# Four expert keys computed ahead in the tail of the routing, and the last table part stored in two halves

## Chip, core and metric

The kernel runs on one core of one Trainium2 chip. The time is the device time of one launch in microseconds (us), and lower is better. The weight matrices, the token rows and the output lie in HBM. A core has five engines with their own instruction streams: PE (TensorE), DVE (VectorE), ACT (ScalarE), POOL (GpSimd) and SP (SyncE, which here only issues DMAs). They meet through semaphores.

## What is computed

One decoder layer on 512 tokens of width 2048: a token mixer (attention beside a recurrence), and then a channel mixer with retrieved experts (PEER). The change touches only the channel mixer:

```python
q = (xt @ w_q).reshape(T, PEER_HEADS, 2, PEER_DHALF)
s = jnp.einsum('thcd,hcnd->thcn', q, sub_keys)
# top 16 of 128 in each half, 256 sums, top 16 of those
eidx = jnp.take_along_axis(cidx, top_pos, axis=-1)
gates = jax.nn.softmax(top_s, axis=-1)
a = jnp.einsum('td,ted->te', xs, u[es])
hact = jax.nn.gelu(a) * gs
return jnp.einsum('te,ted->td', hact, v[es])
```

There are 8 heads, 128 x 128 = 16384 experts, and each token picks 8 x 16 of them.

## The kernel before

For 384 of the 512 tokens the kernel doesn't gather experts. It computes all 16384 densely, and multiplies the activations by a table of gates that is zero where a token did not pick an expert. The experts are walked by their first index, a "key" of 128 experts. The last 128 tokens are done sparsely: POOL gathers the rows of u and of v that they picked (512 KB each time, called a task), and DVE multiplies and sums them.

Every f32 operand of a matmul is split into a high part (ACT, a cast to fp32r) and a low part (POOL or DVE, a subtraction). Each product is three matmuls: high by high, and the two mixed ones.

Three stages follow each other around the change. Each is a block with a stream of its own for each engine, and no engine starts a block before all have finished the one before.

**`route` (L1385 to L1622).** Eight heads. `w_q` is streamed in 512 KB steps, four a head: `Stream` has four raw slots and two slots for the parts; SP loads (L284), ACT makes the high part (`split_high`, L305), POOL the low part (`split_low`, L319, 2.4 us each), PE multiplies (L350 to L352) and releases the parts' slot (`used`). PE then forms the scores (L1459), ACT copies them out (L1492), DVE picks the 16 best and their places (L1537 to L1595), POOL weighs the one-hot places with the indices (`weigh`, L1432) and DVE sums them (`keep`, L1553). PE is done with a head about a head before DVE is. After head 7 DVE subtracts the largest score, ACT takes the exponential (L1519), and DVE divides (L1620 to L1622).

**`gate_table` (L1639 to L1738).** The gates are turned (L1669), and for every 16 tokens DVE (L1699, L1704) and ACT (`match`, L1718 and L1722) build one-hot rows, PE multiplies them (L1678), and ACT copies the result into one of two stages (L1734). 24 rounds of 16 tokens are 6 parts of 64 tokens. When a part is complete, SP stores its stage to `gate_table` in HBM: 4 MB, 32 KB in a row from each partition. The first four raw chunks of the next stage are loaded at the start of this block (`load_first_experts`): u keys 0 and 1.

**`experts` (L1752 to L2034).** 32 macros of four keys. PE does the four u steps (activations of a key: 48 matmuls, L1900 to L1902), then four v steps (output columns, 36 matmuls each, L1919 to L1923). For each key ACT takes the gelu (L1960), DVE multiplies by the gates (L2025), ACT and DVE split the result (L1966, L2030). The gates of a key are a DMA from the table (L1852), 768 pieces of 256 bytes. DVE also makes the low part of every u and v chunk (L1984), adds the output banks into `h` (L2014) and does two sparse tasks per step, 16 a macro, in a written order: in each of 8 steps its splits come first, its additions next, its tasks last. Four row buffers hold gathered rows; a gather (L1879) waits until the task four before it is done. Steps 0 to 7 of the order are named in `SPLITS`: v0, u2, u3, v1, u4, v2, v3, u5; u4 and u5 are the first keys of the next macro.

Of the kernel before, what the change touches and what calls it, by code (L numbers as in the profile page):

```python
# [24 lines left out]
ALU = mybir.AluOpType  # L25
# [237 lines left out]
class Stream:  # L263
# [79 lines left out]
    def parts(self, g, c):  # L343

        return self.hi[:, g % 2, c], self.lo[:, g % 2, c]

# [1035 lines left out]
def route(nc, place, kb, stream, xT, picks, cst, plain_stored):  # L1382


    with ExitStack() as ctx:  # L1385
# [27 lines left out]

        def each_head(eng, head, peeled):
# [7 lines left out]
        @block.sync  # L1422
        def _(sp):
            stream.load_rest(sp, PH)

        @block.gpsimd
        def _(pool):
# [16 lines left out]
            each_head(pool, head, 2)  # L1444
            weigh(PH, 0)
            weigh(PH + 1, 1)

        @block.tensor
        def _(pe):
# [30 lines left out]

            each_head(pe, head, 4)
            scores(PH, 1)

        @block.scalar
        def _(act):
# [8 lines left out]
            def head(m, s, first, last=False):  # L1494
# [6 lines left out]
                if not last:  # L1501
                    stream.split_high(act, m + 1, 0)
# [13 lines left out]
            head(PH - 1, 1, False, True)  # L1516
            empty_scores(PH, 1)
            act.wait_ge(shifted, 1)
            act.activation(picks[2][:, :, :], picks[2][:, :, :], ACT.Exp).then_inc(exp_done, 1)  # L1519

# [112 lines left out]
def gate_table(nc, place, stages, stored, hot, picks, picksT, table, cst, at_turned, sparse):  # L1633
# [5 lines left out]
    with ExitStack() as ctx:  # L1639
# [8 lines left out]
        gaps = place("table_gaps", [P, 2, SLOT_TOKENS, NK], F32, 88)  # L1648
# [5 lines left out]
        @block.sync  # L1654
        def _(sp):
            sp.wait_ge(turned, 3)
            sp.wait_ge(picks_kept, 2)
            at_turned(sp)
            with sp.Fori(0, PARTS // 2) as q:
                for s in range(2):  # L1660
                    sp.wait_ge(banks_out, q * (2 * slots_of_part) + (slots_of_part * (s + 1) + SLOTS))
                    sp.dma_start(table[q * 2 + s], stages[s][:]).then_inc(stored[s], 16)
# [48 lines left out]
        def _(act):  # L1711
# [16 lines left out]
            for q in range(PARTS):  # L1728
                if q >= 2:
                    act.wait_ge(stored[q % 2], 16 * (q // 2))  # L1730
                with act.Fori(0, TABLE_TOKENS // run) as i:
                    for s in range(SLOTS):
# [4 lines left out]
                        if s % 2:  # L1737
                            rounds = TABLE_TOKENS // run * q + 1  # L1738
                            match(s, i * run + rounds * run, i * 2 + (2 * rounds + s // 2 + 1))
# [11 lines left out]
RAW_SLOTS, ROW_SLOTS, NOW = 4, 4, 4  # L1751
SPLITS = (("v", 0), ("u", 2), ("u", 3), ("v", 1), ("u", 4), ("v", 2), ("v", 3), ("u", 5))  # L1752


def experts(nc, place, h, xT, raw, loaded, loads, table, table_stored, out, sparse):
# [11 lines left out]
    with ExitStack() as ctx:  # L1767
# [37 lines left out]

        def split_of(m, step):

            kind, which = SPLITS[step]
# [465 lines left out]
```

## Time and profile before

| what | us |
|---|---|
| median of 3 runs | 3561.41 |
| lowest and highest run | 3547.05, 3562.57 |
| the profiled execution | 3550.87 |
| its span, from first to last instruction | 3549.1 |
| routing's last score matmul begins | 1236.6 |
| table block begins | 1276.3 |
| last table store issued | 1418.0 |
| expert block begins | 1419.9 |
| end of the span | 3549.1 |

Times inside the kernel are counted from the first instruction of the profiled execution, which took 3550.87 us by the same clock as the runs. It is 10.5 us below the median of the three runs. A row of the timeline gives a start, a duration, the engine, the line and what was written from what; a wait ahead of it stands in brackets with the engine that ended it.

### The profile page before, as it was taken

What the parts mean: (1) busy time and instruction counts of PE and PEld (TensorE: products, weight loads), DVE (VectorE), ACT (ScalarE), POOL (GpSimd) and SP (SyncE); (2) the same over time, 40 slices, a digit from 0 to 9 for tenths busy, and PEclk for the clock granted to TensorE, in tenths of its full rate; (3) what the DMA queues carried; (4) which work ended last, traced back from release to release, by engine and by line L of the source; (5) the groups of instructions that cost most, each with busy time, mean ns of one, the idle gap of its engine ahead of it and who ended that gap; (6) DMA issues with size and microseconds to landing.
All of it is one profiled execution on the core that took longest, in us unless ns stands there. A gap on an engine that the chain in (4) does not pass through costs nothing.

```text
span 3549.1 us, 51460 instructions
## 1 busy us (share of the span) xinstructions
PE 3359.0 (95%) x16926; PEld 2944.6 (83%) x16926; DVE 2226.8 (63%) x3877; ACT 1116.9 (31%) x1732; POOL 1165.7 (33%) x870
## 2 busy tenths in 40 slices
PE   7999999878989947999999999999999999999999
PEld 5778876667877746898998998998998998999998
DVE  2003412795028898677777777777777777777776
ACT  3122223443232259322233233222332232222322
POOL 2344431264435410322322323323333333323332
PEclk9999999899999979999999999999999999999999
DMA  4223320002332124888887887888888887888876
GB/s 140 73 87 95 95 83 21 25 1 101 95 107 81 56 94 184 316 265 265 268 267 259 274 265 262 270 265 263 271 264 265 269 267 262 271 267 263 269 262 234
DMA packets 276021, 686.85 MB, mean 194 GB/s; under 512 B 120544, under 2 KB 120800, under 8 KB 273504
## 3 DMA queue, kind: packets, MB, share of 16 engines
q1 hardware_dynamic: 202224, 417.51, 36.3%
q0 software_dynamic: 73728, 268.47, 22.5%
q8 instruction: 38, 0.62, 0.1%
q14 instruction: 31, 0.25, 0.0%
HBM read 655.48 MB, written 30.41 MB: 193 GB/s over the span
## 4 chain that ended last, share of the span: by engine, by line
PE 59%; ACT 2%; issue 1%; DMA 1%; ACTq 0%; DVE 0%; DVEq 0%; SPq 0%
PE exp_a L1900 10%; PE exp_a L1902 10%; PE exp_a L1901 10%; PE exp_o L1921 10%; PE exp_o L1923 10%; PE exp_o L1919 10%; ACT table_gaps L1718 1%; ACT table_stage L1734 1%; DMA gate_table<-table_stage 0%; PE table_b L1678 0%; ACTq L1718 0%; DMA exp_raw<-in_v 0%; ACTq L1734 0%; DVE table_hot L1704 0%; PE table_t L1669 0%
## 5 line engine op out<-in xcount | busy, mean ns | idle before, releaser
L1900 PE MATMUL exp_a<-x_high,exp_uh 128*128 128x384 f32 x2048 | 686.4, 335 | 10.6 <-DVE exp_ul L1984 10.6
L1902 PE MATMUL exp_a<-x_high,exp_ul 128*128 128x384 f32 x2048 | 686.0, 335 | 0.0
L1901 PE MATMUL exp_a<-x_low,exp_uh 128*128 128x384 f32 x2048 | 686.0, 335 | 0.0
L1923 PE MATMUL exp_o<-exp_vh,exp_al 128*128 128x512 f32 x1536 | 598.2, 389 | 0.0
L1921 PE MATMUL exp_o<-exp_vl,exp_ah 128*128 128x512 f32 x1536 | 598.1, 389 | 0.0
L1919 PE MATMUL exp_o<-exp_vh,exp_ah 128*128 128x512 f32 x1536 | 597.5, 389 | 0.0
L1879 POOL DMA_INDIRECT exp_rows<-in_v_rows,exp_now x256 | 329.0, 1285 | 707.9 <-DVE h L2005 656.4
L1879 POOL DMA_INDIRECT exp_rows<-in_u_rows,exp_now x256 | 299.5, 1170 | 733.5 <-DVE exp_rows L1998 688.5
L1949 ACT CAST exp_vh<-exp_raw 128x1024 fp32r<-128x1024 f32 x256 | 260.1, 1051 | 516.4 <-PE exp_o L1923 493.1
L1984 DVE TENSOR_TENSOR exp_vl<-exp_raw,exp_vh 128x1024 fp32r<-128x1024 f32 x256 | 304.5, 1220 | 165.7 <-ACT exp_vh L1949 165.7
L1900 PEld LDWEIGHTS exp_a<-x_high,exp_uh 128*128 128x128 f32 x2048 | 385.8, 188 | 12.3 <-DVE exp_ul L1984 7.3
L1901 PEld LDWEIGHTS exp_a<-x_low,exp_uh 128*128 128x128 f32 x2048 | 385.7, 188 | 1.2
L1902 PEld LDWEIGHTS exp_a<-x_high,exp_ul 128*128 128x128 f32 x2048 | 385.7, 188 | 0.0
L1960 ACT ACTIVATE exp_act<-exp_a 128x384 f32<-128x384 f32 x128 | 63.0, 492 | 963.4 <-PE exp_a L1902 963.4
L1923 PEld LDWEIGHTS exp_o<-exp_vh,exp_al 128*128 128x128 f32 x1536 | 288.4, 188 | 59.9
L1921 PEld LDWEIGHTS exp_o<-exp_vl,exp_ah 128*128 128x128 f32 x1536 | 288.4, 188 | 59.2
L1919 PEld LDWEIGHTS exp_o<-exp_vh,exp_ah 128*128 128x128 f32 x1536 | 288.4, 188 | 59.1
L1984 DVE TENSOR_TENSOR exp_ul<-exp_raw,exp_uh 128x1024 fp32r<-128x1024 f32 x256 | 309.7, 1220 | 41.7 <-ACT exp_uh L1949 31.6
L319 POOL TENSOR_TENSOR w_in_lo<-w_in_raw,w_in_hi 128x1024 fp32r<-128x1024 f32 x88 | 212.7, 2418 | 333.3 <-ACT w_in_hi L305 333.3
L2005 DVE SCALAR_TENSOR_TENSOR h<-exp_rows,exp_weights,h 128x1024 f32<-128x1024 f32 x256 | 316.5, 1276 | 0.0
L1998 DVE SCALAR_TENSOR_TENSOR exp_rows<-exp_rows,sparse_x 128x1024 f32<-128x1024 f32 x256 | 302.2, 1216 | 0.0
L2025 DVE TENSOR_TENSOR exp_act<-exp_act,exp_gates 128x384 f32<-128x384 f32 x128 | 71.8, 561 | 360.3 <-ACT exp_act L1960 360.3
(290 smaller groups left out, 5180.6 us busy)
## 6 DMA issues: line engine op xcount, KB each, us to landing
exp_raw<-in_u SPq DMA_DIRECT2D x256, 512.0 KB, 5.2
exp_raw<-in_v SPq DMA_DIRECT2D x256, 512.0 KB, 4.4
w_in_raw<-in_w_in SPq DMA_DIRECT2D x88, 512.0 KB, 3.6
gate_table<-table_stage SPq DMA_DIRECT2D x6, 4096.0 KB, 11.6
exp_gates<-gate_table SPq DMA_DIRECT2D x128, 192.0 KB, 5.3
w_out_raw<-in_w_out SPq DMA_DIRECT2D x32, 512.0 KB, 3.6
w_q_raw<-in_w_q SPq DMA_DIRECT2D x32, 512.0 KB, 3.9
x_rows<-in_x SPq DMA_DIRECT2D x4, 1024.0 KB, 7.9
```

Source lines behind the costliest of these rows:

```text
L319: eng.tensor_tensor(self.lo[:, g % 2], self.raw[:, g % RAW], self.hi[:, g % 2].bitcast(F32), ALU.subtract).then_inc(self.low, 1)
L1879: pool.indirect_dma_start(rows[slot][:, :], None, sparse["u" if kind == "dot" else "v"], bass.IndirectOffsetOnAxis(ap=now[:, turn, place_n ...
L1900: pe.matmul(bank, uh[:, b, c, :], xh[:, 0:DENSE_TB, c, :], start=(c == 0), stop=False)
L1901: pe.matmul(bank, uh[:, b, c, :], xl[:, 0:DENSE_TB, c, :], start=False, stop=False)
L1902: last = pe.matmul(bank, ul[:, b, c, :], xh[:, 0:DENSE_TB, c, :], start=False, stop=(c == DC - 1))
L1919: pe.matmul(bank[:, :], ah[:, key, tokens], vh[:, dc % 2, key, :], start=(key == 0), stop=False)
L1921: pe.matmul(bank[:, :], ah[:, key, tokens], vl[:, dc % 2, key, :], start=False, stop=False)
L1923: last = pe.matmul(bank[:, :], al[:, key, tokens], vh[:, dc % 2, key, :], start=False, stop=(key == KEYS_OF_MACRO - 1))
L1949: act.copy(part(uh if split[0] == "u" else vh, *split, half), raw[:, c % RAW_SLOTS, :])\
L1984: dve.tensor_tensor(part(ul if kind == "u" else vl, kind, which, half), raw[:, slot, :], part(uh if kind == "u" else vh, kind, which, half ...
L1998: done = dve.scalar_tensor_tensor(rows[slot][:, :], rows[slot][:, :], 1.0, sparse["x"][:, half, :], ALU.mult, ALU.mult, accum_out=dots[:, ...
L2005: done = dve.scalar_tensor_tensor(sums, rows[slot][:, :], weights[:, pl(pick(m, kind, t), 1)], sums, ALU.mult, ALU.add)
```

## The change

The first four u keys are computed in `route`, after head 7. They are further steps of the `w_q` stream (a "head" 8 and 9 of four steps each, a step being half a key). SP loads them, ACT makes eight more high parts, POOL eight more low parts between and behind its last two `weigh`, and PE multiplies them into the four `route_q` banks. ACT's gelu writes the four activations to a new buffer `early_act`. The score matmuls of head 7 stand behind the first half key, ACT's exponential behind all the high parts.

`experts` then starts macro 0 with its v steps. Its first four raw chunks are v columns 0 and 1. DVE multiplies the four activations by their gates, then splits them; POOL's gathers wait until that is done. In `gate_table` the last round has no `match` (it had been computed for tokens that don't exist), and the last of the six parts is stored in two halves of 32 tokens. A half is no longer one run per partition: for each of 16384 pairs of indices it takes 32 of 64 tokens, that is 128 bytes.

```diff
 # route: SP, POOL
+            for key in range(EARLY):
+                for half in range(2):
+                    stream.load_row(sp, *early_step(key, half), u[key, :, half * (D // 2):(half + 1) * (D // 2)])
...
             each_head(pool, head, 2)
+            stream.split_low(pool, *early_step(0, 0))
+            stream.split_low(pool, *early_step(0, 1))
             weigh(PH, 0)
+            stream.split_low(pool, *early_step(1, 0))
+            stream.split_low(pool, *early_step(1, 1))
+            stream.split_low(pool, *early_step(2, 0))
             weigh(PH + 1, 1)
+            stream.split_low(pool, *early_step(2, 1))
+            stream.split_low(pool, *early_step(3, 0))
+            stream.split_low(pool, *early_step(3, 1))
 # route: PE
+            def early_key(key):
+                bank = q_bank[key // 2][key % 2][:, 0:TD].rearrange("p (b t) -> p b t", t=P)
+                pe.wait_ge(q_out, 2 * PH + key - 3)
+                for half in range(2):
+                    p, g = early_step(key, half)
+                    stream.await_step(pe, p, g)
+                    for at in range(DC // 2):
...
+                        last = pe.matmul(bank, low, xh, start=False, stop=(c == DC - 1))
+                    stream.release(last)
+                    if key == 0 and half == 0:
+                        scores(PH, 1)
...
-            scores(PH, 1)
+            for key in range(EARLY):
+                early_key(key)
 # route: ACT, after the eight high parts
             act.wait_ge(shifted, 1)
             act.activation(picks[2][:, :, :], picks[2][:, :, :], ACT.Exp).then_inc(exp_done, 1)
+            for key in range(EARLY):
+                open_early(key)
 # gate_table: SP
-                    sp.dma_start(table[q * 2 + s], stages[s][:]).then_inc(stored[s], 16)
+            for q in range(PARTS):
+                pieces = 2 if q == PARTS - 1 else 1
+                count = TABLE_TOKENS // pieces
+                for k in range(pieces):
+                    sp.wait_ge(banks_out, slots_of_part * q + slots_of_part // pieces * (k + 1) + SLOTS)
+                    tokens = slice(k * count, (k + 1) * count)
+                    sp.dma_start(table[q][:, :, tokens], stages[q % 2][:, :, tokens]).then_inc(stored[q % 2], 16)
 # experts: POOL, ACT, DVE
+            pool.wait_ge(a_split, EARLY)
             run(pool, macro)
...
-                act.copy(part(uh, "u", n // 2, n % 2), raw[:, n, :]).then_inc(high, 1)
+                act.copy(part(vh, "v", n // 2, n % 2), raw[:, n, :]).then_inc(high, 1)
+            for key in range(EARLY):
+                act.wait_ge(weighted, key + 1)
+                act.copy(ah[:, key, :], early[:, key, :]).then_inc(a_high, 1)
...
-                low_part("u", n // 2, n % 2, n, n + 1)
+                low_part("v", n // 2, n % 2, n, 2 * EARLY + n + 1)
+            for key in range(EARLY):
+                dve.wait_ge(gates_in[key % 2], 16 * (key // 2 + 1))
+                dve.tensor_tensor(early[:, key, :], early[:, key, :], gates[:, key % 2, :], ALU.mult)\
+                    .then_inc(weighted, 1)
+            for key in range(EARLY):
+                dve.wait_ge(a_high, key + 1)
+                dve.tensor_tensor(al[:, key, :], early[:, key, :], ah[:, key, :].bitcast(F32),
+                                  ALU.subtract).then_inc(a_split, 1)
```

What stands in a row on POOL at the end of the routing, before (`route_hot` is a `weigh`, the branch the end of the block):

```order
217 L318 REGISTER_ALU
218 L319 TENSOR_TENSOR w_q_lo<-w_q_raw,w_q_hi 128x1024
219 L1418 REGISTER_ALU
220 L1418 COMPARE_AND_BRANCH
221 L1432 TENSOR_TENSOR route_hot<-route_hot,route_idx_f 128x1024 x4
222 L1385 UNCONDITIONAL_BRANCH
```

and now:

```order
219 L1439 REGISTER_ALU
220 L1439 COMPARE_AND_BRANCH
221 L319 TENSOR_TENSOR w_q_lo<-w_q_raw,w_q_hi 128x1024 x2
222 L1456 TENSOR_TENSOR route_hot<-route_hot,route_idx_f 128x1024 x2
223 L319 TENSOR_TENSOR w_q_lo<-w_q_raw,w_q_hi 128x1024 x3
224 L1456 TENSOR_TENSOR route_hot<-route_hot,route_idx_f 128x1024 x2
225 L319 TENSOR_TENSOR w_q_lo<-w_q_raw,w_q_hi 128x1024 x3
226 L1402 UNCONDITIONAL_BRANCH
```

Three low parts of the early keys stand behind the last `weigh`, with the matmuls that need them.

On ACT at the same place, before:

```order
411 L1506 COPY route_qT<-route_q 128x512
412 L1508 COPY route_qT<-route_q 128x512
413 L1492 COPY route_scores<-route_s 128x512 x2
414 L1519 ACT_TABLE_LOAD
415 L1519 ACTIVATE picks_80<-picks_80 128x512
416 L1385 UNCONDITIONAL_BRANCH
```

and now:

```order
411 L1556 COPY route_qT<-route_q 128x512
412 L1558 COPY route_qT<-route_q 128x512
413 L305 CAST w_q_hi<-w_q_raw 128x1024
414 L1543 COPY route_scores<-route_s 128x512 x2
415 L305 CAST w_q_hi<-w_q_raw 128x1024 x6
416 L1581 ACT_TABLE_LOAD
417 L1581 ACTIVATE picks_80<-picks_80 128x512
418 L1569 ACT_TABLE_LOAD
419 L1569 ACTIVATE early_act<-route_q 128x384 x4
420 L1402 UNCONDITIONAL_BRANCH
```

Six high parts and a second load of function tables stand around the exponential, and the four gelus behind it.

On DVE at the start of the expert block and in macro 0, now (`exp_dots` are the sparse tasks, `h` the additions of output banks):

```order
726 L2073 TENSOR_TENSOR exp_vl<-exp_raw,exp_vh 128x1024 x4
727 L2143 TENSOR_TENSOR early_act<-early_act,exp_gates 128x384 x4
728 L2147 TENSOR_TENSOR exp_al<-early_act,exp_ah 128x384 x4
729 L2087 SCALAR_TENSOR_TENSOR exp_rows_9797,exp_dots<-exp_rows_9797,sparse_x 128x1024
...
736 L2087 SCALAR_TENSOR_TENSOR exp_rows_9800,exp_dots<-exp_rows_9800,sparse_x 128x1024
737 L2073 TENSOR_TENSOR exp_ul<-exp_raw,exp_uh 128x1024 x2
738 L2087 SCALAR_TENSOR_TENSOR exp_rows_9797,exp_dots<-exp_rows_9797,sparse_x 128x1024
739 L2087 SCALAR_TENSOR_TENSOR exp_rows_9798,exp_dots<-exp_rows_9798,sparse_x 128x1024
740 L2073 TENSOR_TENSOR exp_vl<-exp_raw,exp_vh 128x1024 x2
741 L2103 TENSOR_TENSOR h<-h,exp_o 128x512 x3
```

Between the early keys' split (row 728) and the low parts of v2 (row 740) there are ten tasks and the low parts of u4; before, the splits and the gate products of keys 2 and 3 stood between the same tasks.

## Rows read from the trace of the kernel before

**Rows 1.** The page: the span, and the busy share of the engines.

```profile
span 3549.1 us, 51460 instructions
PE 3359.0 (95%) x16926; PEld 2944.6 (83%) x16926; DVE 2226.8 (63%) x3877; ACT 1116.9 (31%) x1732; POOL 1165.7 (33%) x870
```

**Rows 2.** Busy time by stretch; PEclk is the granted clock, 1.00 is 2.4 GHz.

```profile
core 0: us, PE busy (x) PEld busy (x) DVE busy (x) ACT busy (x) POOL busy (x), PEclk, DMA share, GB/s
1241.00:1272.00 31.00, 0.00 (x0) 0.00 (x0) 26.91 (x117) 0.63 (x1) 9.73 (x4) 0.54 0.00 0
1282.00:1420.00 138.00, 101.48 (x768) 92.29 (x768) 128.14 (x428) 134.87 (x343) 0.09 (x1) 0.97 0.42 175
1445.00:1511.00 66.00, 65.65 (x326) 60.03 (x327) 51.83 (x74) 19.64 (x25) 21.89 (x19) 0.97 0.86 295
```

**Rows 3.** What PE waited for: us in total, times, longest.

```profile
PE table_t L1669 <- PEq L1385: 37.8, 1, 37.8
PE exp_a L1900 <- DVE exp_ul L1984: 10.6, 2, 7.1
```

**Rows 4.** Timeline of the routing's end, engine by engine.

```profile
1236.62 2.05 PE L1459 MATMUL route_s<-sub_keys,route_qT 128*128 128x128 f32 x16
1238.71 0.58 ACT L1492 COPY route_scores<-route_s 128x512 f32<-128x512 f32 x1 [0.31 <-PE route_s L1459]
1239.32 1.28 ACT L1519 ACT_TABLE_LOAD   x1
1269.64 0.63 ACT L1519 ACTIVATE picks<-picks 128x512 f32<-128x512 f32 x1 [29.04 <-DVE picks L1616]
1225.81 2.40 POOL L319 TENSOR_TENSOR w_q_lo<-w_q_raw,w_q_hi 128x1024 fp32r<-128x1024 f32 x1 [0.41 <-ACT w_q_hi L305]
1266.72 5.08 POOL L1432 TENSOR_TENSOR route_hot<-route_hot,route_idx_f 128x1024 f32<-128x1024 f32 x2 [18.66 <-DVE route_hot L1595]
1243.24 1.64 DVE L1537 MAX8 route_val<-route_scores 128x8 f32<-128x128 f32 x8
1276.32 0.29 DVE L1685 SCALAR_TENSOR_TENSOR sparse_experts<-picks,picks 128x128 uint32<-128x128 f32 x1 [0.31 <-PEq L1385]
```

**Rows 5.** Timeline of the table's end.

```profile
1414.90 1.28 ACT L1718 ACTIVATE table_gaps<-c_iota,table_minus 128x128 f32<-128x128 f32 x4
1416.75 1.05 ACT L1734 COPY table_stage<-table_b 128x512 f32 x2
1414.11 1.16 PE L1678 MATMUL table_b<-table_hot 128*128 128x128 f32 x8 [0.74 <-ACT table_hot L1722]
1395.66 22.65 SPq L1662 DMA_DIRECT2D gate_table<-table_stage  x2
1417.97 0.33 SPq L1662 DMA_DIRECT2D gate_table<-table_stage  x1
1431.67 0.82 SPq L2204 DMA_DIRECT2D exp_raw<-in_v  x2
```

**Rows 6.** DMA queues, issues with median us to landing, and shortest landings (gates, gathers).

```profile
q1 hardware_dynamic: 202224, 417.51, 36.3%
q0 software_dynamic: 73728, 268.47, 22.5%
gate_table<-table_stage SPq DMA_DIRECT2D x6, 4096.0 KB, 11.6
c_ln_mix<-in_ln_mix SPq DMA_DIRECT2D x1, 8.0 KB, 2.5
DMA to landing us min/median/max: 3.6/5.3/11.5
DMA to landing us min/median/max: 4.3/5.4/11.7
```

**Rows 7.** Timeline of the experts' start.

```profile
1422.37 0.69 PE L1900 MATMUL exp_a<-x_high,exp_uh 128*128 128x384 f32 x1 [7.11 <-DVE exp_ul L1984]
1427.98 0.35 PE L1902 MATMUL exp_a<-x_high,exp_ul 128*128 128x384 f32 x1
1463.72 0.49 ACT L1960 ACTIVATE exp_act<-exp_a 128x384 f32<-128x384 f32 x1 [5.53 <-PE exp_a L1902]
1496.20 0.33 PE L1900 MATMUL exp_a<-x_high,exp_uh 128*128 128x384 f32 x1
```

**Rows 8.** The page's groups: busy, mean ns of one.

```profile
L1949 ACT CAST exp_vh<-exp_raw 128x1024 fp32r<-128x1024 f32 x256 | 260.1, 1051 | 516.4 <-PE exp_o L1923 493.1
L1984 DVE TENSOR_TENSOR exp_vl<-exp_raw,exp_vh 128x1024 fp32r<-128x1024 f32 x256 | 304.5, 1220 | 165.7 <-ACT exp_vh L1949 165.7
L1998 DVE SCALAR_TENSOR_TENSOR exp_rows<-exp_rows,sparse_x 128x1024 f32<-128x1024 f32 x256 | 302.2, 1216 | 0.0
L2025 DVE TENSOR_TENSOR exp_act<-exp_act,exp_gates 128x384 f32<-128x384 f32 x128 | 71.8, 561 | 360.3 <-ACT exp_act L1960 360.3
```

More of the change, by code:

```diff
@@ L1492, in empty_scores, with head @@
                     act.copy(sc[:, 2 * s + k], s_bank[s][k][:, :, :]).then_inc(s_out, 1)
-            def head(m, s, first, last=False):
+            def head(m, s, first):
                 if not (first and m == 0):
@@ L1500, in head @@
                 stream.split_high(act, m, 3)
-                if not last:
-                    stream.split_high(act, m + 1, 0)
+                stream.split_high(act, m + 1, 0)
                 act.wait_ge(q_done, m + 1)
@@ L1730, in _, with empty @@
                     act.wait_ge(stored[q % 2], 16 * (q // 2))
-                with act.Fori(0, TABLE_TOKENS // run) as i:
+                rounds = TABLE_TOKENS // run
+                def empty(i, with_match):
                     for s in range(SLOTS):
@@ L1736, in _ @@
                             .then_inc(banks_out, 1)
-                        if s % 2:
-                            rounds = TABLE_TOKENS // run * q + 1
-                            match(s, i * run + rounds * run, i * 2 + (2 * rounds + s // 2 + 1))
+                        if s % 2 and with_match:
+                            begun = rounds * q + 1
+                            match(s, i * run + begun * run, i * 2 + (2 * begun + s // 2 + 1))
+                last = q == PARTS - 1
+                with act.Fori(0, rounds - last) as i:
+                    empty(i, True)
+                if last:
+                    empty(rounds - 1, False)
 HALF_D = D // 2
@@ L1751, with experts @@
 RAW_SLOTS, ROW_SLOTS, NOW = 4, 4, 4
+STORES = PARTS // 2, PARTS // 2 + 1
+EARLY_STEPS = range(4)
 SPLITS = (("v", 0), ("u", 2), ("u", 3), ("v", 1), ("u", 4), ("v", 2), ("v", 3), ("u", 5))
[L1755 removed]
+def experts(nc, place, h, xT, raw, loaded, loads, table, table_stored, out, sparse, early):
     xh, xl = xT
@@ L1928, in macro @@
             def macro(m, kind):
-                for key in range(KEYS_OF_MACRO):
-                    u_step(m, key)
+                if not is_first(m):
+                    for key in range(KEYS_OF_MACRO):
+                        u_step(m, key)
                 for dc in range(D // PC):
                     v_step(m, dc)
+            pe.sem_inc(a_done, EARLY)
             run(pe, macro)
@@ L1955, in macro @@
                     done = m * KEYS_OF_MACRO + (key + 1)
-                    after_u = 0 <= key < KEYS_OF_MACRO
+                    after_u = 0 <= key < KEYS_OF_MACRO and not is_first(m)
                     if after_u:
@@ L2020, in macro @@
                     done = m * KEYS_OF_MACRO + (key + 1)
-                    after_u = 0 <= key < KEYS_OF_MACRO
+                    after_u = 0 <= key < KEYS_OF_MACRO and not is_first(m)
                     if after_u:
```

67 lines of the change are left out of this document (49 added, 18 removed).

## The prediction

> **What bounds the kernel now.** I read four views. The page first: PE is busy for 95% of the span [rows 1]. The stretches next: a macro of the expert stage, 66 us, has PE busy for 65.65 us and DVE for 51.83 [rows 2]. So whatever delays the start of that chain of macros delays the end by as much, and whatever PE is spared there is won. Then what PE waited for: once for 37.8 us, at the end of the routing, and for 10.6 us at the start of the experts [rows 3]. Last the timelines around those waits [rows 4, 5, 7]. In the first one PE's last score matmul starts at 1236.62, DVE picks for head 7 until about 1266.7, POOL's last `weigh` ends at 1271.8, and the next block starts at 1276.32 [rows 4]. In the table block ACT is the bound (134.87 of 138 us) and PE has work for 101.48 [rows 2].
>
> The measure of the change is one point: when macro 0's last v step ends and key 0 of macro 1 starts. It is 1496.20 before [rows 7]. From there on the two kernels do the same, with PE full.
>
> **What is removed.** The four u steps of macro 0. PE starts them at 1422.37, and ACT takes the gelu of the fourth at 1463.72 [rows 7]; the v steps fill 1463.7 to 1496.2, 32.5 us, 8.13 each. The chain from the last table copy (ended 1417.80 [rows 5]) to the first v step is 45.9 us, and all of it is to be replaced.
>
> **The routing's tail.** DVE's path: the scores now follow the first half key. 24 matmuls take half of a warm u step; four such steps and the v steps fill a macro's 66 us, so a u step is (66.0 - 32.5) / 4 = 8.4 and a half 4.1 to 4.2. The scores end 4.1 later, at 1242.8, and ACT's second copy ends at about 1243.4 instead of 1239.3; DVE came free at 1243.24 [rows 4]. That costs 0.25 us.
>
> POOL's path is longer. Its last `weigh` starts at 1267.0 and ends at 1272.05; three low parts of 2.40 [rows 4] stand behind it. By then PE has done five half keys: the first three low parts behind the earlier `weigh` are ready by 1258.3. PE has stood idle from about 1264.5. The next steps form a chain, because there are only two slots for the parts and two low parts of 2.40 must come before:
> - low part of (2,1): 1272.05 to 1274.45;
> - PE's half key (2,1): cold. The first matmul at 1422.37 came after 7 us of waiting with a clock of 1.2 GHz, and it was 5.6 us until the first short one, at 1427.98, the 18th [rows 7]; so 24 matmuls are 5.6 + 7 x 0.17 = 6.9 us, to 1281.4;
> - ACT's high part of (3,1), which needs that slot: 1.05, to 1282.5. POOL's low part: to 1284.9. PE: (3,0) to 1285.6 and (3,1) to 1289.7;
> - ACT behind that high part: table load 1.28, exponential 0.63, table load 1.28, three gelus, to 1287.1, and the last gelu at 1289.8 to 1290.3. DVE's division, 2 us behind the exponential, is done by 1286.5 and is covered.
>
> The block ends at 1290.3 instead of 1276.0, that is 14.3 us later: not POOL's 3 x 2.4, but the round trip through the slot. The idle 37.8 us of PE hide the first 27 us of the four keys, no more. What comes back: PE enters the table block warm, where it was cold. ACT's first rounds waited for it, about 1 us. I take 13.3 net; bounds 7 (if only the three low parts count) and 18 (all of PE's four last halves cold).
>
> **The table's end.** ACT drops the `match` between the last two copies: four squares in 1.28 and a Relu in 0.63. The last PE group ended at 1415.27 [rows 5], so the last copy ends at 1416.0 instead of 1417.80: 1.8 won. Last copy after the change: 1417.8 + 13.3 - 1.8 = 1429.3.
>
> **The store in halves.** Before, the last 4 MB were issued at 1417.97 and SP went on at 1431.67, 13.7 us [rows 5], with gathers beside it; the median of the six is 11.6 [rows 6]. Afterwards half 1 can be issued at 1420, but part 4's store, issued at 1395.66 + 13.3 = 1409.0 by the same shift, takes its 11.6 + 1 first, so the halves' data start at 1421.5. They have 2 x 16384 runs of 128 bytes, 2048 for each of 16 engines. No row shows such a store. The two queues give a price per packet: 16 engines' span is 56786 us; 73728 packets and 268.47 MB took 22.5% of it, 202224 and 417.51 MB took 36.3% [rows 6]. Solved for both, that is 8.5 ns a packet and 0.045 ns a byte, 14.3 ns for 128 bytes. The gates give another: 192 KB in runs of 256 bytes land in 3.6 us at least, 8 KB in 2.5 [rows 6]; 1.1 us for 48 packets an engine is 23 ns, less 128 x 0.045 = 17 ns. The second is a transfer of the same kind, short runs by the thousand, so I take 17: 2048 x 17 = 34.8 us. The data are then in at S = 1456.3, 27.0 us behind the last copy where it was 13.8. Bounds: no charge for the cut at all (half 2 lands 7 us behind the last copy, S = 1436), and twice 17 ns (69.6 us, S = 1491).
>
> The Trainium skill, DMA: Bandwidth & Descriptors, section Specifications, speaks against this edit: below 512 bytes a transfer is no longer at line rate because the DMA engine reads, modifies and writes. No row here has a short run into HBM; the gates are short runs out of it.
>
> **From S to the first v step.** Nothing of macro 0 can be weighted before S. ACT makes four high parts of v and DVE four low ones (1.05 and 1.22 [rows 8]): DVE is through at S + 5.8. Gates 0 and 1 are in by then. Gates 2 are issued when buffer 0 is free (S + 6.4) and land 3.8 later; gates 3 behind them and behind the first load of u4, at S + 12. The four splits of the activations stand behind all four products (0.56 each [rows 8]): the first low part is ready at S + 13.1, the last at S + 14.5. PE's first v step starts at S + 13.2.
>
> **Inside macro 0.** PE is cold again and loses 2.6 us in its first step (by the 5.6 us above). Two v steps end at S + 13.2 + 16.3 + 2.6 = S + 32.1. The third needs v2's low part. POOL's gathers now begin at S + 14.6, a first one lands 5.5 later (1.2 for the indices, 4.3 [rows 6]), and on DVE ten tasks come before v2 (order of the change, rows 729 to 740). Tasks 0 to 3 end at S + 25.7; with four row buffers each later gather starts when its task four before is done, so tasks 4 to 7 end 5.7 later, S + 31.4. Then two low parts of u4 (2.3), two tasks (2.3), two low parts of v2 (2.3), a third of the bank addition (0.6): S + 38.9. PE waits 6.8 us and is cold once more, 2.6. Macro 0 ends at S + 38.9 + 16.3 + 2.6 = S + 57.8.
>
> **Sum.** 1456.3 + 57.8 = 1514.1 against 1496.2: 17.9 us later. In parts: tail +14.3, warm start -1.0, `match` -1.8, last copy to first v step 27.0 + 13.2 = 40.2 for 45.9 (-5.7), two cold starts +5.2, the wait for DVE +6.8; together +17.8. The profiled execution would take 3550.87 + 18 = 3569. The median of the runs is 10.5 us above that execution, so against it I forecast 3561.4 + 18 = 3579.
>
> **Rivals.**
> 1. The cut of the store is nearly free (about 5 us a half, as for 2 MB of the 11.6 us row). S = 1436 and the sum is 18 - 20 = -2: 3559, not slower. For it: the store of 4 MB moves in large packets at full rate, and a long stream may hide a packet's fixed cost. Against: the queues' price per packet. It decides as soon as a packet costs under about 7 ns.
> 2. Cheap packets: 14.3 ns, S = 1450.8, and a tail 3 us shorter: +9, 3570. Not to be told from no change.
> 3. A short run written to HBM costs a read and a write, 34 ns: S = 1491, +53, 3614. That is what the page named above would make of it.
> 4. The v2 wait does not come (tasks keep up because the DMA queues are empty): 6.8 + 2.6 less, +9, 3570. For it: PE's clock may hold over a short wait. Against: the tasks' order is written out.
>
> **How the numbers follow.** About 0.5%, 18 us, is what a measurement of this kernel can tell from no change. Forecast (17 to 24 ns a packet, with its tail): 0.45, from +12 to +30. Rival 1: 0.10. Rivals 2 and 4: 0.25. Rival 3: 0.20. My forecast sits on the bound: a little over half of its 0.45 lies above. Slower: 0.28 + 0.20 + 0.04 = 0.52. Faster needs -18, which even rival 1 does not give: 0.04. The rest, 0.44, is no change. The range takes rivals 1, 2 and 4, the forecast, and rival 3 up to its middle: 3556 to 3614.
>
> **What would show it.** In the changed profile: the table block starts near 1290 (7 us earlier: POOL alone sets the tail). The two half stores take some 15 to 18 us each in a row after part 4's; 5 each is rival 1, over 30 each is rival 3. SP's first gates are issued near 1456. PE's first v matmul comes 13 us after that. PE waits once inside macro 0, before the third v step, for DVE. Key 0 of macro 1 starts near 1514. I am wrong if PE's wait moved elsewhere, above all if the clock stays low through the tail, or if macros after the first no longer have PE full.

## The result, and the profile of the changed kernel

The changed kernel takes 3565.4 us (median of 20 runs, 3554.9 to 3573.2), the kernel before 3552.8 (20 runs, 3540.2 to 3563.4). The ratio is 1.0034 with a 95% interval of 1.0021 to 1.0046: 12.6 us slower (7.5 to 16.3). That is clear of zero, but below the 0.5% that the forecast called measurable. The forecast was 3579 against a median of three runs that twenty runs put 8.6 us lower; as a difference it was +18, and +12.6 came. The direction and the order of the waits held, the size did not.

The page of the changed kernel, its span, busy time and queues:

```profile
span 3562.8 us, 51412 instructions
PE 3369.4 (95%) x16926; PEld 2951.2 (83%) x16926; DVE 2219.1 (62%) x3869; ACT 1114.5 (31%) x1722; POOL 1194.0 (34%) x878
q1 hardware_dynamic: 234880, 417.51, 37.1%
gate_table<-table_stage SPq DMA_DIRECT2D x5, 4096.0 KB, 11.6
gate_table<-table_stage SPq DMA_DIRECT2D x2, 2048.0 KB, 15.5
```

Against [rows 1] the span is 13.7 us longer, and against [rows 6] the queue has 32656 packets more: the last 4 MB went in 32768 packets of 128 bytes.

**First the part that is not the change's.** The last `route_qT` copy of the routing is the last instruction that both kernels reach by the same work. (Only ACT's first early high part stands ahead of it, at 1237.10, and ACT then still waits for PE.) ACT takes the copy at 1236.67 before and here at

```profile
1242.48 0.59 ACT L1558 COPY route_qT<-route_q 128x512 f32<-128x512 f32 x1
```

that is, 5.8 us of the 13.7 are there before anything changed. They go with PE's granted clock in the recurrence and attention. Two stretches, of before and then of after (PE, PEld, DVE, ACT, POOL busy, granted clock, DMA share, GB/s):

```profile
650.00:860.00 210.00, 165.41 (x1023) 143.49 (x1022) 172.81 (x330) 85.78 (x217) 102.64 (x125) 0.89 0.07 21
860.00:1020.00 160.00, 155.09 (x691) 128.28 (x689) 14.79 (x28) 42.37 (x65) 69.25 (x29) 1.00 0.37 122
```

```profile
650.00:860.00 210.00, 165.73 (x1000) 144.69 (x1000) 171.75 (x328) 83.88 (x215) 102.01 (x124) 0.86 0.06 21
860.00:1020.00 160.00, 160.00 (x720) 132.76 (x719) 12.90 (x20) 42.01 (x61) 71.66 (x30) 1.00 0.37 118
```

PE is as busy as before in the first stretch, but at 0.86 for 0.89; in the second, work still fills the 5 us in which before had already run dry. Over the thirteen profiled executions of this study that copy came anywhere from 1234.0 to 1251.6, with the same code before it. The earliest (e7, below) and the latest (e11) in the same columns:

```profile
640.00:1230.00 590.00, 526.15 (x2674) 440.42 (x2675) 353.74 (x1138) 190.61 (x376) 277.43 (x198) 0.95 0.23 74
```

```profile
640.00:1230.00 590.00, 526.35 (x2602) 440.66 (x2601) 340.79 (x1062) 186.37 (x371) 269.59 (x193) 0.92 0.22 71
```

The same busy time, a clock of 0.95 and 0.92, and 72 matmuls between them. So from here on I count every time from this copy (the mark). On the other side nothing scatters: from key 0 of macro 1 to the end of the span it is 2052.9 us before, 2052.8 after, and one or the other in all eleven variants.

**Then the change's own part.** Counted from the mark, key 0 of macro 1 starts at 259.5 before (1496.20 [rows 7]) and at 267.5 after (1509.96): **+8.0 us**. What PE waits for now (the short waits inside the table block, 34 us in total before and 33 now, are left out):

```profile
PE exp_o L2001 <- DVE exp_al L2147: 30.4, 1, 30.4
PE route_q L1524 <- POOL w_q_lo L319: 13.3, 2, 9.5
PE exp_o L2001 <- DVE h L2103: 10.2, 1, 10.2
PE table_t L1736 <- PEq L1402: 1.0, 1, 1.0
```

The 37.8 us at the end of the routing [rows 3] are down to 1.0; two waits, 13.3 together, for POOL's low parts remain inside the tail. The 10.6 us at the experts' start became 30.4 before the first v step and 10.2 before the third. The chain that ended last leads through these (start, us, what):

```profile
1431.40 1.54 ACT table_stage L1803 x3
1432.94 0.50 ACTq L1703
1433.46 16.85 DMA gate_table<-table_stage
1450.33 1.05 ACT exp_vh L2062
1451.41 4.63 DVE exp_vl L2073 x4
...
1457.54 4.37 DMA exp_gates<-gate_table
1461.93 0.56 DVE early_act L2143
1462.49 1.87 DVE exp_al L2147 x4
1464.36 5.97 issue
1470.41 1.25 DVE exp_rows L2087 x2
...
1482.59 5.24 DMA exp_rows<-in_u_rows,exp_now
1487.85 1.23 DVE exp_rows L2087 x2
1489.08 2.27 DVE exp_vl L2073 x2
1491.36 0.61 DVE h L2103
1492.10 0.76 PE exp_o L2001
```

Read from the top: the last four table copies (the timeline has them end at 1433.43), the store of the second half with 16.85 us to its landing, ACT's and DVE's parts of v, the gates of the early keys and their split; then DVE has nothing until the first gathered rows, and its backlog of tasks holds the low parts of v2, and with them PE.

### The profile page after: what moved, and what is told of

Its sections match the earlier page's. It is cut to its first block, busy times and chain, and to the rows that moved or that the text cites. A ratio compares the mean times of both kernels' runs of the same rounds, so it can differ in the third digit from the quotient of the medians.

```text
span 3562.8 us, 51412 instructions
## 1 busy us (share of the span) xinstructions
PE 3369.4 (95%) x16926; PEld 2951.2 (83%) x16926; DVE 2219.1 (62%) x3869; ACT 1114.5 (31%) x1722; POOL 1194.0 (34%) x878
## 4 chain that ended last, share of the span: by engine, by line
PE 58%; ACT 2%; issue 1%; DVE 1%; DMA 1%; ACTq 0%; POOL 0%; DVEq 0%; SPq 0%; POOLq 0%
PE exp_a L1982 10%; PE exp_a L1984 10%; PE exp_a L1983 10%; PE exp_o L2003 10%; PE exp_o L2005 10%; PE exp_o L2001 10%; ACT table_gaps L1785 1%; ACT table_stage L1803 0%; DMA gate_table<-table_stage 0%; PE table_b L1745 0%; DVE table_hot L1771 0%; DVE exp_vl L2073 0%; DMA exp_rows<-in_u_rows,exp_now 0%; ACTq L1785 0%; POOL exp_rows L1963 0%
## 5 line engine op out<-in xcount | busy, mean ns | idle before, releaser
L1984 PE MATMUL exp_a<-x_high,exp_ul 128*128 128x384 f32 x1984 | 663.1, 334 | 0.0
L1982 PE MATMUL exp_a<-x_high,exp_uh 128*128 128x384 f32 x1984 | 663.0, 334 | 0.0
L1983 PE MATMUL exp_a<-x_low,exp_uh 128*128 128x384 f32 x1984 | 662.9, 334 | 0.0
L2001 PE MATMUL exp_o<-exp_vh,exp_ah 128*128 128x512 f32 x1536 | 599.4, 390 | 40.6 <-DVE exp_al L2147 30.4
L1982 PEld LDWEIGHTS exp_a<-x_high,exp_uh 128*128 128x128 f32 x1984 | 372.4, 188 | 1.2
L1983 PEld LDWEIGHTS exp_a<-x_low,exp_uh 128*128 128x128 f32 x1984 | 372.4, 188 | 1.2
L1984 PEld LDWEIGHTS exp_a<-x_high,exp_ul 128*128 128x128 f32 x1984 | 372.4, 188 | 0.0
L2073 DVE TENSOR_TENSOR exp_ul<-exp_raw,exp_uh 128x1024 fp32r<-128x1024 f32 x248 | 300.2, 1221 | 31.3 <-ACT exp_uh L2033 31.3
L2087 DVE SCALAR_TENSOR_TENSOR exp_rows<-exp_rows,sparse_x 128x1024 f32<-128x1024 f32 x256 | 303.0, 1219 | 10.2 <-DMA exp_rows<-in_u_rows,exp_now 10.0
## 6 DMA issues: line engine op xcount, KB each, us to landing
gate_table<-table_stage SPq DMA_DIRECT2D x5, 4096.0 KB, 11.6
```

The lines of the kernel that those rows point to most:

```text
L1982: pe.matmul(bank, uh[:, b, c, :], xh[:, 0:DENSE_TB, c, :], start=(c == 0), stop=False)
L1983: pe.matmul(bank, uh[:, b, c, :], xl[:, 0:DENSE_TB, c, :], start=False, stop=False)
L1984: last = pe.matmul(bank, ul[:, b, c, :], xh[:, 0:DENSE_TB, c, :], start=False, stop=(c == DC - 1))
L2001: pe.matmul(bank[:, :], ah[:, key, tokens], vh[:, dc % 2, key, :], start=(key == 0), stop=False)
L2073: dve.tensor_tensor(part(ul if kind == "u" else vl, kind, which, half), raw[:, slot, :], part(uh if kind == "u" else vh, kind, which, half ...
L2087: done = dve.scalar_tensor_tensor(rows[slot][:, :], rows[slot][:, :], 1.0, sparse["x"][:, half, :], ALU.mult, ALU.mult, accum_out=dots[:, ...
```

## The experiments

All times in the table are us behind the mark. "Table" is the first DVE work on the table block that depends on the picks (`picksT` copied), S is the issue of the first gates, V the first v matmul, and M the start of key 0 in macro 1, on which the end depends. One profiled execution stands behind each line; the single executions differ by up to 17.6 us ahead of the mark, so their whole times are not compared.

| kernel | table | S | V | M | M against after |
|---|---|---|---|---|---|
| before | 40.9 | 196.3 | 226.8 | 259.5 | -8.0 |
| after | 53.6 | 207.9 | 220.6 | 267.5 | |
| e1 last part whole | 53.8 | 202.3 | 215.0 | 263.3 | -4.2 |
| e2 runs of 256 B | 53.8 | 212.2 | 225.0 | 273.2 | +5.7 |
| e3 runs of 64 B | 53.7 | 241.3 | 254.3 | 301.7 | +34.3 |
| e4 two low parts first | 47.5 | 202.2 | 215.1 | 263.5 | -4.0 |
| e5 before, with halves | 41.0 | 203.5 | 232.7 | 265.3 | -2.2 |
| e6 twelve parts | 53.6 | 197.4 | 210.7 | 259.0 | -8.5 |
| e7 eight tasks ahead | 53.7 | 212.7 | 233.1 | 268.7 | +1.2 |
| e8 one low part first | 49.7 | 203.7 | 216.1 | 263.9 | -3.6 |
| e9 all together | 47.5 | 191.9 | 208.4 | 242.8 | -24.7 |
| e10 before, twelve parts | 41.0 | 189.9 | 221.7 | 254.4 | -13.1 |
| e11 e4 and e6 | 47.5 | 191.6 | 205.0 | 252.5 | -15.0 |

### What the cut of the last part costs (e1, e5, e2, e3)

**e1_whole**: the changed kernel with its last part stored in one piece.

```diff
...
-                for k in range(pieces):
-                    sp.wait_ge(banks_out, slots_of_part * q + slots_of_part // pieces * (k + 1) + SLOTS)
-                    tokens = slice(k * count, (k + 1) * count)
-                    sp.dma_start(table[q][:, :, tokens], stages[q % 2][:, :, tokens]).then_inc(stored[q % 2], 16)
+                sp.wait_ge(banks_out, slots_of_part * (q + 1) + SLOTS)
+                sp.dma_start(table[q], stages[q % 2][:]).then_inc(stored[q % 2], 16)
```

> The changed kernel with one edit undone: the last table part is stored whole again, 4 MB in 32 KB runs, issued at the last copy (nothing else is in the queue then). Theory 'the cut costs': in the changed kernel the last half landed 16.9 us behind the last copy; whole, it lands 11.7 us behind it (the other five stores take 11.6 to 11.8), so the experts start 5.2 us earlier and key 0 of macro 1 stands 5 us earlier against the routing. Rival 'the halves help': a half is 2 MB and lands earlier than the whole; then this kernel is later by up to 5 us.

**e5_halves_before**: the kernel before with the store in halves, and nothing else (the reverse of the diff above, in the old loop).

> The other edit alone: the kernel before, with only the last table part stored in two halves (128-byte runs). There four gathers of 512 KB and the first two u keys run beside the store. Theory 'the cut costs, beside other traffic too': two halves take 24.1 us of data alone where the whole takes 10.3, half 1 starts 11 us before the last copy, and the gathers' 2 MB queue in; SP goes on 17 to 21 us behind the last copy instead of 13.9, PE waits for v0's chunks and u2 by as much longer, and key 0 of macro 1 is 3 to 7 us later than in the kernel before. Rival 'an early half helps where other traffic waits behind 32 KB packets': the gathers slip between short packets, SP goes on no later than before, and the time doesn't change.

Measured: whole, S is 5.6 earlier and M 4.2. The chain of e1 has in the same place

```profile
1426.21 11.12 DMA gate_table<-table_stage
1437.35 1.05 ACT exp_vh L2058
```

11.12 us from issue to the next step for 16.85. In the kernel before, the halves cost 5.8 at M: SP goes on 202.1 behind the mark (1436.71) where it went on at 195.0, and PE waits 15.4 for `exp_ul` in place of 10.6:

```profile
1436.71 0.82 SPq L2207 DMA_DIRECT2D exp_raw<-in_v  x2
PE exp_a L1903 <- DVE exp_ul L1987: 15.4, 2, 8.3
```

So storing in halves, meant to bring the last landing forward, is a loss of 4 to 6 us in either kernel: half of the change's +8.

**e2_runs256** and **e3_runs64** measure the packet. In e2 the last part goes out behind the last copy in two transfers, each taking every other run of 64 tokens (two times 8192 runs of 256 bytes); in e3 in four of 16 tokens each (four times 16384 runs of 64 bytes). The bytes are the same 4 MB.

```diff
...
+                    for k in range(2):
+                        sp.dma_start(table[q].rearrange("i (a b) t -> i a b t", b=2)[:, :, k, :],
+                                     stages[q % 2][:].rearrange("i (a b) t -> i a b t", b=2)[:, :, k, :])\
...
```

> Measures the price of short runs by itself: the last part is stored after its last copy, in two DMAs that take every second 256-byte run (16384 runs of 256 bytes, 1024 an engine, instead of 32768 of 128 bytes). In the changed kernel 2048 packets an engine took 24.1 us, 11.8 ns each. If the price is per packet, whatever its size up to 256 bytes, the data take 12 us. If it is 8.5 ns plus 0.045 a byte, as the prediction had it, 20 ns each and 20.5 us. If it is by the byte (174 GB/s for any short run), 24 us.

> The same with runs of 64 bytes: the last part is stored after its last copy in four DMAs of 16 tokens each, 65536 runs, 4096 packets an engine. Per packet at 11.8 ns: 48 us. By the prediction's two queues, 8.5 + 2.9 = 11.4 ns each: 47 us. By the byte: 24 us. If a short write to HBM costs a read and a write of a larger piece, more than 48 us. Key 0 of macro 1 moves by as much.

The stretches in which only these stores move, of after, e2 and e3:

```profile
1430.00:1448.00 18.00, 1.97 (x16) 1.59 (x14) 0.00 (x0) 3.40 (x8) 0.00 (x0) 0.60 1.65 174
```

```profile
1440.00:1450.00 10.00, 0.00 (x0) 0.00 (x0) 0.00 (x0) 0.00 (x0) 0.00 (x0) 0.50 0.96 217
```

```profile
1430.00:1470.00 40.00, 0.00 (x0) 0.00 (x0) 0.00 (x0) 0.00 (x0) 0.00 (x0) 0.50 1.88 88
```

The last number is GB/s, over 16 engines. 128 bytes at 174 / 16 = 10.9 GB/s take 11.8 ns; 64 bytes at 5.5 GB/s take 11.6; 256 bytes at 13.6 GB/s take 18.9. Between 64 and 128 bytes the price of a packet hardly changes, and only their number counts. These 11.8 ns are what the forecast had at 17, and at 34 in its third rival, "a read and a write". That rival put S 62 us behind the last copy (1491 for 1429.3); 17.0 came. Whether a read is made at all no row says; if there is one, its price is within these 11.8 ns. The rival took its reason from the Trainium skill (DMA: Bandwidth & Descriptors, section Specifications), which puts transfers under 512 bytes below line rate. The trace agrees with that: 174 GB/s at 128 bytes and 217 at 256, for 419 in long runs (below). The doubling of 17 ns was the rival's own.

The same 4 MB in one piece, in e1, move at 419 GB/s:

```profile
1427.00:1437.00 10.00, 0.00 (x0) 0.00 (x0) 0.00 (x0) 0.00 (x0) 0.00 (x0) 0.50 0.98 419
```

So at 128 bytes each half takes about 12 us, 24 for both, where 4 MB in one piece take 10, and the first half's head start of 9.3 us (issued at 1424.12 and 1433.46) is not enough.

### What the routing's tail costs (e4, e8)

**e4_tail2** puts the low parts of (2,1) and (3,0) ahead of POOL's last `weigh`; **e8_tail1** only the first of them.

```diff
             stream.split_low(pool, *early_step(2, 0))
-            weigh(PH + 1, 1)
             stream.split_low(pool, *early_step(2, 1))
             stream.split_low(pool, *early_step(3, 0))
+            weigh(PH + 1, 1)
             stream.split_low(pool, *early_step(3, 1))
```

> The changed kernel with POOL's order in the routing's tail changed: the low parts of half keys (2,1) and (3,0) stand before the last weigh, where POOL was idle for 6.7 us, only that of (3,1) behind it. Theory 'slot round trip behind weigh': PE's half key (2,1) starts at once behind (2,0), warm; the last weigh starts 1.6 us later, the block ends with the last gelu about 8 us earlier than in the changed kernel, and everything behind it too. Rival 'DVE and weigh set the tail': the block ends at most 1 us earlier, or later by the 1.6 us.

> As e4_tail2, but only the low part of (2,1) is moved ahead of the last weigh; those of (3,0) and (3,1) stand behind it. e4 brought the table's start 6.1 us forward. Theory 'slot round trip': the last weigh starts as in the changed kernel, (3,0) waits for POOL until 5.1 + 2.4 us after it began, (3,1) 2.4 later; the block ends 5 us earlier than in the changed kernel. Rival 'the whole gain of e4 came from (2,1) and the rest is DVE': 6.1 here as well.

First the tail of after, POOL and then ACT:

```profile
1272.70 5.08 POOL L1456 TENSOR_TENSOR route_hot<-route_hot,route_idx_f 128x1024 f32<-128x1024 f32 x2 [6.71 <-DVE route_hot L1659]
1277.74 4.67 POOL L319 TENSOR_TENSOR w_q_lo<-w_q_raw,w_q_hi 128x1024 fp32r<-128x1024 f32 x2
1287.37 2.40 POOL L319 TENSOR_TENSOR w_q_lo<-w_q_raw,w_q_hi 128x1024 fp32r<-128x1024 f32 x1 [4.95 <-ACT w_q_hi L305]
```

```profile
1286.23 1.05 ACT L305 CAST w_q_hi<-w_q_raw 128x1024 fp32r<-128x1024 f32 x1 [14.43 <-PE route_q L1526]
1287.31 1.28 ACT L1581 ACT_TABLE_LOAD   x1
1288.60 0.63 ACT L1581 ACTIVATE picks<-picks 128x512 f32<-128x512 f32 x1
1289.25 1.28 ACT L1569 ACT_TABLE_LOAD   x1
1294.50 0.49 ACT L1569 ACTIVATE early_act<-route_q 128x384 f32<-128x384 f32 x1 [2.70 <-PE route_q L1526]
```

This is the round trip of the forecast: ACT's high part of (3,1) waits for PE to free the slot, POOL stands 4.95 us for that high part, and the last gelu follows PE. POOL had idled 6.71 us ahead of its last `weigh`: room for two low parts. e4 uses it: the table block starts 6.1 earlier and PE's 13.3 us fall to 6.8. The 6.1 are less than the 8 expected. At M only 4.0 of the 6.1 arrive: 5.7 are left at S, 5.5 at V, and 4.6 at the third v step, before which PE now waits 11.5 for DVE instead of 10.2:

```profile
PE exp_o L2001 <- DVE h L2103: 11.5, 1, 11.5
PE route_q L1524 <- POOL w_q_lo L319: 6.8, 2, 3.9
```

e8 brings 4.0 at the table, where 5 were expected, and 3.6 at M. Between the two orders M does not tell.

### The backlog of tasks (e7)

**e7_tasks_ahead** takes away what made the gathers wait: ACT copies `early_act` to a buffer of its own, POOL waits for that copy and not for the split, and DVE does the first eight tasks of macro 0 ahead of the low parts of v, while the table is still being stored.

```diff
+TASKS_AHEAD = 8
...
-            pool.wait_ge(a_split, EARLY)
+            pool.wait_ge(moved, EARLY)
...
+            for key in range(EARLY):
+                act.copy(kept[:, key, :], early[:, key, :]).then_inc(moved, 1)
...
+            for t in range(TASKS_AHEAD):
+                task(0, "dot", t)
```

> The changed kernel with eight sparse tasks of macro 0 done while the table's last part is being stored: ACT copies early_act to the low parts' place first, so the gathers' buffers are free, POOL gathers at once, and DVE does tasks 0 to 7 ahead of v's low parts. Theory 'DVE's task order is what PE waits for in macro 0': PE's wait of 10.2 us before the third v step and its cold clock behind it (2.6) go; but 4 MB of gathers share the DMA engines with the store, so the first gates come up to 8 us later. Net 3 to 12 us earlier. Rival 'the wait is the output banks or v2's chunk': PE's wait stays, and the time gets longer by the store's delay.

The wait before the third v step is gone from the list, and from V to M it now takes 35.6 us for 46.9. Still nothing is won, for V is 12.5 later, and so M is 1.2 later, where 3 to 12 us earlier were expected. POOL's first gather, then rows of DVE: the first task, the eighth, and the low parts behind them.

```profile
1431.68 1.14 POOL L1966 DMA_INDIRECT exp_rows<-in_u_rows,exp_now  x1 [0.96 <-POOL exp_now L1961]
1439.85 1.23 DVE L2092 SCALAR_TENSOR_TENSOR exp_rows<-exp_rows,sparse_x 128x1024 f32<-128x1024 f32 x1 [19.83 <-DMA exp_rows<-in_u_rows,exp_now]
...
1453.83 1.23 DVE L2092 SCALAR_TENSOR_TENSOR exp_rows<-exp_rows,sparse_x 128x1024 f32<-128x1024 f32 x1 [1.08 <-DMA exp_rows<-in_u_rows,exp_now]
1454.98 0.08 DVE L2092 DVE_READ_ACCUMULATOR exp_rows<-exp_rows,sparse_x 128x1 f32 x1
1454.98 4.63 DVE L2078 TENSOR_TENSOR exp_vl<-exp_raw,exp_vh 128x1024 fp32r<-128x1024 f32 x4
```

Of DVE's 19.83 us of waiting the larger part passes before POOL issues a gather at all: POOL waits for ACT's copies, and these for the end of the table block. From there it is 8.2 us to the first task beside the store in short runs, for 4.8 in the changed kernel (1465.58 to 1470.41). The eighth task ends at 1454.98, 8.3 behind SP's first gates (1446.70), and the low parts, which are the way to V, stand behind it. S itself is 4.8 later. This run shows that PE waited for the backlog of tasks, that it can be moved and that eight tasks are too many. What the wait is worth by itself it does not show, as the gathers also slowed the store.

### Smaller parts of the table (e6, e10, e11)

**e6_parts32** has twelve parts of 32 tokens, each stored whole, so that the last store is 2 MB in one run a partition; **e10_before_parts32** is the same in the kernel before. The price could lie in the gates, whose runs halve to 128 bytes in all 32 macros.

```diff
-TABLE_TOKENS = 64
+TABLE_TOKENS = 32
...
```

> The changed kernel with twelve table parts of 32 tokens instead of six of 64: every part is one run of 16 KB per partition, 2 MB, and the last one is issued at the last copy. The gates of a key are then 1536 runs of 128 bytes instead of 768 of 256. Theory: a 2 MB store in long runs lands about 6.5 us behind the last copy (the 4 MB took 11.6, 1.3 of it fixed), not 16.9; gates take at most 0.2 to 1 us longer at 11.8 ns a packet; key 0 of macro 1 is 9 to 10 us earlier than in the changed kernel. Rival 'short gate runs cost it back': each macro's four gate loads take the queues twice as long and PE no longer has its chunks in time, seen as waits of PE in every macro.

> The kernel before with twelve table parts of 32 tokens and nothing else. The last store is 2 MB in long runs and SP goes on 4 to 6 us earlier behind it; v0 and u2 come earlier, and PE's waits of 3.5 us before key 2, with 1.6 us of cold clock behind it, go. Theory: key 0 of macro 1 is 3 to 5 us earlier than in the kernel before, all that this wait is worth, since PE then works through its four u steps. Rival 'gate loads in 128-byte runs cost it back': no gain, or PE waits in every macro.

e6: S is 10.5 earlier than after and M 8.5: the last store takes 6.3 us where the last half took 16.85 (the median of the twelve is 6.4). The gates cost nothing. 660 us of later macros, e6 and before:

```profile
2000.00:2660.00 660.00, 660.00 (x3363) 603.45 (x3362) 485.84 (x644) 191.25 (x241) 202.60 (x181) 1.00 0.83 266
```

```profile
2000.00:2660.00 660.00, 660.00 (x3363) 603.50 (x3362) 485.82 (x640) 191.40 (x242) 201.89 (x181) 1.00 0.81 266
```

PE is busy without a gap in both, with the DMA share at 0.83 for 0.81. In e10 M is 5.2 earlier than in before; its twelve runs are 7.5 us below the kernel before, with a ratio of 0.9985 and an interval of 0.997 to 1.0, so by the runs alone it is no more than likely.

**e11_tail2_parts32** is e4 and e6 in one.

> e9 without the tasks' move: the new tail order and the twelve parts. If the three terms add, key 0 of macro 1 stands at 252 to 254 behind the routing's last query copy, and PE still waits 10 us before the third v step. If it is that wait which takes up the gains, it stands at 256 or more, with a wait of 13 us or more.

M is 15.0 earlier than after's, where the two alone gave 4.0 and 8.5. At V the terms add up (5.5 and 9.9 alone, 15.6 together); the 2.5 us more at M arise in macro 0's v steps, and no run says why. PE still waits 10.3 before the third v step. Against the kernel before that is -7.0 at M.

### Together (e9)

**e9_all** is e4 and e6, with e7's move cut to four tasks, which DVE takes while it waits for gates: two behind the product of key 1, two behind that of key 2.

```diff
+TASKS_AHEAD = 4
...
                 dve.tensor_tensor(kept[:, key, :], kept[:, key, :], gates[:, key % 2, :], ALU.mult)\
                     .then_inc(weighted, 1)
+                if key in (1, 2):
+                    task(0, "dot", 2 * key - 2)
+                    task(0, "dot", 2 * key - 1)
```

> The changed kernel with three mends together: low parts of (2,1) and (3,0) ahead of the last weigh (e4), twelve parts of 32 tokens stored whole (e6), and the first gathers of macro 0 issued at once, with four tasks done where DVE waits for the gates of keys 2 and 3 instead of behind the splits (of e7 only what doesn't stand in the way of v's low parts). Against the routing's last query copy, key 0 of macro 1 stood at 259.5 us in the kernel before and at 267.5 in the changed one. If the terms add: 267.5 - 5.5 (tail) - 8.5 to -10.5 (store) - 6 to -11 (PE's wait before the third v step, with its cold clock) + 1 to 3 (gathers beside the store) = 242 to 248, so 11 to 17 us below the kernel before, 0.3 to 0.5%. Rival 'the terms hide each other': the wait for DVE takes up what the tail and store give (as it took up 2 us of the 5.6 in e4), and it stands above 253.

PE now waits last before the first v step; no wait before the third is left:

```profile
PE exp_o L2000 <- DVE exp_al L2154: 23.9, 1, 23.9
```

V is 3.4 later than in e11 (208.4 for 205.0), for the four tasks, and M 9.7 earlier: macro 0's v steps take 34.4 us instead of 47.5. M is 16.7 us ahead of before. The twelve runs have a median of 3540.6 (3529.0 to 3548.5) against 3553.0 for before on the same chip: ratio 0.9963, interval 0.9947 to 0.9979. That is faster than the kernel before, if by less than 0.5%. Of the 16.7, the twelve parts are worth 5.2 in the kernel before too (e10); the other 11.6 are what the early keys bring once their store, their order on POOL and their queue on DVE are right. As the change was written, these three made it lose 8.

## Why the prediction was right or wrong

Its steps, with the time from the mark; the rows of before are [rows 4, 5 and 7].

| step | forecast | measured |
|---|---|---|
| start of the table block (1276.32 to 1295.29, less 5.8) | +14.3 | +13.2 |
| table block, last copy (1417.80 to 1433.43, less 5.8 and 13.2) | -2.8 | -3.4 |
| last copy to S (part of the line after next) | 27.0 | 17.0 |
| S to first v step (part of the next line) | 13.2 | 12.7 |
| last copy to first v step, against 45.9 | -5.7 | -16.2 |
| two cold starts (measured: what is left of macro 0's time) | +5.2 | +4.2 |
| wait for DVE before the third v step | +6.8 | +10.2 |
| **key 0 of macro 1** | **+17.8** | **+8.0** |

**The step that failed is the packet price.** The forecast had two numbers for it, 14.3 ns from the two queues and 17 from the gates, and took 17 "as a transfer of the same kind, short runs by the thousand". It was 11.8: 24 us for both halves, not 34.8. The 10.0 us in "last copy to S" are the whole miss of 9.8 and a little more; the other steps missed by -1.1, -0.6, -0.5, -1.0 and +3.4, which nearly cancel. That they cancel is luck. Both estimates took a price out of times that hold other things. The gates' 3.6 us less the 2.5 of a tiny transfer come from 48 packets an engine and not from thousands, and no row told a rate in them from a latency; and the queues' busy shares count the time from a packet's start to its end, while packets overlap on an engine (the share of the stretch 1430 to 1448 is 1.65). The lower of the two was the nearer. The gates were called the same kind of transfer for their short runs, although they are reads and few. Rival 2 had cheap packets and a shorter tail at +9: its packet half came, at a price still below its 14.3; its tail came only in part (1.1 us of 3). That its sum is near the measured +8.0 is luck.

**The tail was right, with its reason.** It was not 7 us (three low parts) but the round trip through the slot: 13.2 for 14.3, with the instructions of the chain about 1 us from where the text puts it (ACT's high part of (3,1) at 1286.23 less 5.8 = 1280.4, forecast 1281.4; POOL's last low part 1281.6, forecast 1282.5). PE's cold half key took 6.1 us (1280.14 to 1286.2) for 6.9. e4 and e8 show it by moving it.

**The table block** gave 3.4 back for 2.8 (the dropped `match` and the warm start). The split between the two was not measured.

**From S to the first v step** everything is in its place (12.7 for 13.2).

**The wait for DVE came, and larger.** It stands where the forecast had it, before the third v step, for the low parts of v2 and the bank addition `h` behind them, which ends last. The first task starts 20.0 behind S (forecast 20.1) and the fourth ends at 26.0 (25.7); the eighth ends at 33.6 (31.4), and the ninth and tenth lose another 0.5 to their rows. The later gathers share the queues with the first loads of macro 0; that this delays them is likely, but no run separated it. Third v step at S + 41.7, forecast 38.9; and V being 0.5 earlier adds to the wait. Rival 4 is out: without those tasks in the way (e9) the wait goes, with them it stays.

**The baseline.** The forecast added 18 to a median of three runs, 3561.4. Twenty runs put it at 3552.8. Single runs of before differ by up to 23 us. In the thirteen traces the scatter lies ahead of the mark (17.6 us), where the clock differs, and none lies in the last 2053 us; three runs could not average it out. It changes the forecast time and not the difference: of the 14.0 us by which 3579.4 was too high, 8.6 are the baseline and 5.4 the change.

**What stays open.** The trace has +8.0 for the change and the runs +12.6, with 8.0 inside their interval (7.5 to 16.3). e9 has -16.7 in the trace and -12.4 in the runs, while e10, without the keys, has -5.2 and -7.5. The two kernels with the early keys are thus some 4 us slower in the runs than at M, and the mark of the ten profiled executions with them lies at 1242.3 in the mean, that of the three without at 1236.6. That would fit if the new kernels came to the mark a little later, although their code up to there is the same. Three executions without the keys are too few to show it, and no run separated it. How much of the gap between traces and runs is only this is not settled.

## What to carry to other kernels

Before cutting a store to overlap its first half, count the runs of the halves: here 4 MB as 128 runs took 10 us and as 32768 runs took 24, and the cut lost 4 to 6 us; smaller whole parts got the overlap without it. Work moved into a stage's idle time has to be placed on every engine that feeds it: PE's 38 us were free, but POOL's order and the two slots for parts made the routing end 13 us later, and the queue of DVE that had been covered by the removed steps turned into a new wait. And when single runs scatter by more than the effect, pick the last instruction ahead of the change that both kernels share, and measure from it.

## What the runs showed of the hardware that was not expected

- Short runs written to HBM cost 11.6 ns a packet and engine at 64 bytes, 11.8 at 128 and 18.9 at 256, that is 88, 174 and 217 GB/s over 16 engines, for 419 GB/s in runs of 32 KB. From 64 to 128 bytes the price hardly changes. No store here has runs between 256 bytes and 16 KB, so where full rate begins was not measured, nor whether a read goes before the write.
- PE's granted clock in one and the same stretch of the same code was 0.89 in one execution and 0.86 in another, and the point at its end moved over 17.6 us in thirteen executions. From key 0 of macro 1 on, the same executions agree within 0.1 us.
- A gather beside a store in short runs is slower: 8.2 us from POOL's first gather to the task on its rows in e7, for 4.8 in the changed kernel.
- Stores in short runs hold SP back. The four stores of e3 wait for nothing of the program after the first, and yet their issue took until 1461.5, 35.6 us; what SP waited for no row says:

```profile
1425.91 35.61 SPq L1729 DMA_DIRECT2D gate_table<-table_stage  x4
```
